# A moving operand's high and low parts laid side by side: one run of 512 values where there were two of 256

## The reference

```python
def first_block(...):
    h = concatenate([m, x], axis=1)
    h = h + hybrid_mixer(rmsnorm(h, norm_mix), w_in, ..., w_out)
    h = h + swiglu(rmsnorm(h, norm_ffn), w_gate, w_up, w_down)
    return rmsnorm(h, final_norm)[:, N_META:]

def second_block(...):
    h = x @ w_in                    # q, k, v, u and two gates
    ...
    merged = sigmoid(gate_attn) * y_attn + sigmoid(gate_pool) * y_pool
    x = layer_norm(ALPHA * x + merged @ w_out)
    return layer_norm(ALPHA * x + square(relu(x @ w_ff1)) @ w_ff2)
```

## Time and profile before

| | |
|---|---|
| median of 3 runs | 2449.61 us (2449.36 to 2449.77) |
| the profiled execution: time, span | 2449.89 us, 2447.8 us |
| TensorE matmuls, busy | 2433.8 us, 99%, 14762 matmuls |
| VectorE, busy | 1614.5 us, 66% |
| ScalarE, busy | 1202.2 us, 49% |
| GpSimd, busy | 173.9 us, 7% |
| share of the SP queue's transfers | 58.8% of 16 DMA engines |
| read from HBM | 445.12 MB |

### The profile page before, as it was taken

How to read it: one execution, slowest core, us unless ns; L and a number is a source line. 1 busy time by engine, 2 the same in 40 slices (tenths; PEclk the granted TensorE clock), 3 DMA queues, 4 the chain that set the end, 5 groups by cost and what they waited for, 6 DMA issues and landing times.

```text
span 2447.8 us, 36417 instructions
## 1 busy us (share of the span) xinstructions
PE 2433.8 (99%) x14762; PEld 2173.7 (89%) x14762; DVE 1614.5 (66%) x2518; ACT 1202.2 (49%) x1728; POOL 173.9 (7%) x195
## 2 busy tenths in 40 slices
PE   8999999999999999999999999999999999999999
PEld 8999998888888888888888888888998888888887
DVE  5646676676666666667677756678885665565667
ACT  6545545544544543455555654544554443443544
POOL 0001111000000000002211102031110000000010
PEclk9999999999999999999999999999999999999999
DMA  7554456666566666665655455565566666656663
GB/s 250 180 161 139 141 165 189 200 184 194 182 198 190 189 190 189 192 190 185 197 188 167 166 185 190 184 193 186 162 196 193 189 189 189 194 190 189 183 193 117
DMA packets 125751, 449.59 MB, mean 184 GB/s; under 512 B 13840, under 2 KB 16400, under 8 KB 125584
## 3 DMA queue, kind: packets, MB, share of 16 engines
q1 hardware_dynamic: 125296, 446.91, 58.8%
q10 hardware_dynamic: 288, 0.36, 0.0%
HBM read 445.12 MB, written 2.10 MB: 183 GB/s over the span
## 4 chain that ended last, share of the span: by engine, by line
PE 96%; DVE 2%; ACT 1%; issue 0%; DMA 0%; ACTq 0%
PE out_bank L614 28%; PE out_bank L618 27%; PE out_bank L615 14%; PE out_bank L617 14%; PE out_bank L622 3%; PE out_bank L621 3%; PE out_bank L623 3%; DVE w_lo L1307 1%; ACT w_hi L895 0%; PE side_bank L734 0%; PE side_bank L694 0%; PE side_bank L749 0%; PE side_bank L725 0%; DVE h L1824 0%; DMA h<-in_tokens 0%
## 5 line engine op out<-in xcount | busy, mean ns | idle before, releaser
L1307 DVE TENSOR_TENSOR w_lo<-raw,w_hi 128x1024 fp32r<-128x1024 f32 x839 | 1037.4, 1240 | 601.0 <-ACT w_hi L895 596.9
L895 ACT CAST w_hi<-raw 128x1024 fp32r<-128x1024 f32 x840 | 878.1, 1049 | 953.6 <-PE out_bank L618 874.8
L614 PE MATMUL out_bank<-a_op,w_hi 128*128 128x512 f32 x1984 | 784.2, 395 | 0.5 <-DVE h L1334 0.3
L618 PE MATMUL out_bank<-a_op,w_hi 128*128 128x512 f32 x1984 | 776.7, 391 | 0.0
L615 PE MATMUL out_bank<-a_op,w_lo 128*128 128x256 f32 x1984 | 558.8, 282 | 0.0
L617 PE MATMUL out_bank<-a_op,w_lo 128*128 128x256 f32 x1984 | 552.0, 278 | 0.0
L617 PEld LDWEIGHTS out_bank<-a_op,w_lo 128*128 128x128 f32 x1984 | 380.1, 192 | 84.3
L615 PEld LDWEIGHTS out_bank<-a_op,w_lo 128*128 128x128 f32 x1984 | 372.9, 188 | 77.0
L614 PE MATMUL out_bank<-b_op,w_hi 128*128 128x512 f32 x992 | 389.7, 393 | 0.0
L618 PE MATMUL out_bank<-b_op,w_hi 128*128 128x512 f32 x992 | 388.0, 391 | 0.0
L614 PEld LDWEIGHTS out_bank<-a_op,w_hi 128*128 128x128 f32 x1984 | 373.1, 188 | 2.0 <-DVE w_lo L1307 0.7
(11 more groups left out here) (302 smaller groups left out, 1974.6 us busy)
## 6 DMA issues: line engine op xcount, KB each, us to landing
raw<-in_w_ff SPq DMA_DIRECT2D x256, 512.0 KB, 4.2
raw<-in_w_in SPq DMA_DIRECT2D x223, 512.0 KB, 3.7
raw<-in_w_gu SPq DMA_DIRECT2D x176, 512.0 KB, 4.2
raw<-in_w_down SPq DMA_DIRECT2D x88, 512.0 KB, 4.3
raw<-in_w_out SPq DMA_DIRECT2D x64, 512.0 KB, 4.3
raw<-in_w_ba SPq DMA_DIRECT2D x16, 512.0 KB, 3.9
raw<-in_w_bp SPq DMA_DIRECT2D x16, 512.0 KB, 3.8
out<-h SPq DMA_DIRECT2D x8, 256.0 KB, 2.3
```

Of the source, the lines that this page charges most:

```text
L614: t_.e.matmul(bank[:, :], wh, a_both, start=start, stop=False, skip_group_check=True)
L618: mm = t_.e.matmul(bank[:, :], wh, a_both, start=False, stop=stop, skip_group_check=True)
L895: a.e.copy(w_hi[:, m % SPLIT, :], raw[:, u % RAW, :]).then_inc(hi_split)
L1307: v_.e.tensor_tensor(w_lo[:, m % SPLIT, :], raw[:, u % RAW, :], w_hi[:, m % SPLIT, :].bitcast(F32), ALU.subtract).then_inc(lo_split)
```

## The change

In `a_late` the low part's 256 columns now lie directly behind the high part's. The high rows of both K tiles of a slot begin where they began (values 48 and 564 of the slot); the low rows begin at values 304 and 820 instead of 306 and 822. The 512-column in-products of the late stages read one run of 512 values; those of 256 columns read the high row as before. `b_op`, the early stages, the count and the order of all instructions and all waits are the same.

```diff
+        def side_by_side(kt, i):
+
+            at = PLACE + ROW * 2 * (kt % 2) + SEQ * i
+            return a_late[:, kt // 2, at:at + SEQ * (2 - i)]
+
             def moving(blk, cols, kt):
 
                 if blk.operand == "a" and blk.stage not in ("k", "f", "q", "v", "conv"):
-                    return part(a_late, kt, 0), part(a_late, kt, 1), parts(a_late, kt)
+                    return side_by_side(kt, 0)[:, 0:SEQ], side_by_side(kt, 1), side_by_side(kt, 0)
...
-                            v_.e.scalar_tensor_tensor(part(a_late, j, 1), h[:, j, REAL], p_col(gain, j),
+                            v_.e.scalar_tensor_tensor(side_by_side(j, 1), h[:, j, REAL], p_col(gain, j),
                                                       part(a_late, j, 0).bitcast(F32), ALU.mult,
                                                       ALU.subtract).then_inc(norm_split)
...
-                v_.e.tensor_tensor(part(a_late, j, 1), src, part(a_late, j, 0).bitcast(F32),
+                v_.e.tensor_tensor(side_by_side(j, 1), src, part(a_late, j, 0).bitcast(F32),
                                    ALU.subtract).then_inc(merged_split)
...
-                    v_.e.tensor_tensor(part(a_late, slot, 1), work[slot % 4][:, 0:SEQ],
+                    v_.e.tensor_tensor(side_by_side(slot, 1), work[slot % 4][:, 0:SEQ],
                                        part(a_late, slot, 0).bitcast(F32), ALU.subtract).then_inc(ff_split)
```

## The result

The changed kernel takes **2472.69 us** (2472.51 to 2472.86, 3 runs) against 2449.61 us: 23.1 us slower, a ratio of 1.0094 with a 95% interval of 1.0071 to 1.0117. The forecast was no change, and the time lies 15.7 us above the range.

The account below looks back on a forecast made before the run. The prediction took TensorE's own pace to bound the kernel, 1856 cycles of 693.3 ns being 53% of the span. Its terms summed 0 + 0 + 0, so it forecast no change, 2449.6 us, with a range of 2438 to 2457 us.

Parts of the forecast that it names:

- What bounds the kernel, and the pace of a cycle: TensorE, busy 2433.8 of 2447.8 us, sets the time; 1856 affected cycles of four in-products take 693.3 ns each.
- something other than the layout: Suspected if the second operand's stages or `q`, which the change leaves alone, did not keep 693 ns a cycle.
- Point 1: TensorE's 512-column reads become one run: a jump costs at most 2.4 ns, saving up to 8.8 us; taken as 0.
- The bound from the one-run reads of `k`: Stage `k`'s 272-column one-run matmuls have 12.1 ns excess each, leaving at most 4.7 ns a cycle for two jumps.
- Point 2: Low rows of the late operand begin 8 bytes earlier: a start's place was said not to matter; taken as 0.
- Point 3: VectorE writes the low rows 8 bytes earlier: at worst 5.6 us if slower and uncovered; taken as 0.
- point 4: What would bind next: were TensorE 1% faster, no other bound, such as the making of weights, would be met.
- Rival B: TensorE's moving-operand and weight reads fall on each other otherwise: 7 ns a cycle slower, 2462.6 us; chance 0.15.
- the sign that only the gaps of 512 columns would carry the loss: In TensorE's starts, a gain or loss should show in each 512-column gap and not in the 256-column ones.
- Rival A: Each jump in TensorE's long reads costs 2.4 ns: 2440.8 us, chance 0.17; far more, under 2438, chance 0.07.
- Rival C: TensorE joins or splits runs itself, so 8 bytes are nothing to it: forecast time; chance 0.61 together with the forecast.
- The lines of 16 bytes: SBUF said to be read in 16-byte lines; one line fewer per low row would save 6.6 us; not adopted.

Follow-up runs that it names:

- e1: The changed kernel with only the even K tiles' low rows directly behind the high ones, the odd ones keeping their 8-byte jump: 2473.02 us.
- e2: The changed kernel with only the odd K tiles' low rows directly behind the high ones, the even ones keeping their 8-byte jump: 2473.11 us.
- e3: The changed kernel with all low rows 16 bytes behind the end of the high ones, so two runs per long read: 2463.06 us.
- e10: The changed kernel with the odd K tile's rows 16 bytes earlier (2240, 3264), all long reads still in one run: 2449.2 us.
- e7: The changed kernel with 64 bytes of padding ahead of the weight buffers: 2479.56 us.
- e8: The kernel before the change with 64 bytes of padding ahead of the weight buffers: 2496.54 us.
- e13: The changed kernel with 128 bytes of padding ahead of the weight buffers, the column of `minus` placed in the padding: 2439.29 us.
- s2_scan: The changed kernel with seven late-operand layouts, one for each time it is written; 693.3 ns a cycle in `gu`, 686.7 in steady `out2`; no total given.
- e12: The changed kernel with every row of the late operand 128 bytes earlier (starts 64 and 2128): 2438.67 us.

## Why the prediction was wrong

- *What bounds the kernel, and the pace of a cycle*: right. TensorE's own pace was the whole matter, 1856 cycles carried it, and the other operand kept its pace. `q` kept its time, but not its pace at every moment (700.0 ns where 693.2 had been read), which the prediction had named as a sign of something other than the layout.
- *Point 1, the jump costs between 0 and 2.4 ns*: wrong in kind. The jump has no price of its own. It moves the low row, and that made -6.7 or +3.3 ns a jump at the two places tried. The bound from the one-run reads of `k` compared two widths at two places as if they were two forms of reading, and so was no bound.
- **Point 2 is the step that failed**: "Three layouts, two kinds of alignment, two lengths of jump, one pace: I take 0 here too." The term was put at 0 and measured 13.3 ns a cycle over 1856 cycles. Of the three layouts, two are the same (late layout and `b_op`), and `q` was read on 19 cycles that end where its pace goes to 700. Moved by 64 bytes against the weights, the kernel before goes at 710.0. A place that two stages share is one sample, not two. Behind it stood a tacit assumption, that only alignment within the row could matter; nothing asked where the weights lie.
- *Point 3 and point 4*: right; no wait on the low parts' writes appeared, and at 686.8 ns nothing else came to bind.
- *Rival B* had the mechanism, reads of the moving operand and of the weights that fall on each other otherwise, and the warning sign, single gaps that differ between `gu` and `q`. Its price, 7 ns a cycle (up to 10), was half of the 13.3 measured; it had been given a chance of 0.15. The reason against it, that the low half lies behind the weight load, fell with e1 and e2: 8 bytes in one low row move the gaps of all kinds of in-product, those of 256 columns too (115.0 to 123.3 ns in e2). So did the sign that only the gaps of 512 columns would carry the loss: in the changed kernel 4.5 of the 13.3 ns are in the others.
- *Rival A* as a fixed price is refuted by e3 and e10. *Rival C* is refuted by the result.
- One rule that bears on rival B was not weighed. By the Trainium skill (TensorE: Matmul & The Clock Gate, Part 2, step 1), moving operand and weight load have read ports of their own, and loading the next tile's weights takes no read bandwidth from the running matmul. By that rule no padding ahead of the weights should change a pace, yet the pace of `gu` went from 706.6 to 700.1 ns (e7), from 693.3 to 710.0 (e8) and from 706.6 to 686.8 (e13). The measurement decides: the two reads are not independent here.
- The lines of 16 bytes that the prediction took from the Trainium skill (Advanced Engine Details and Errata, Memory Cachelines) don't tell fast from slow: e3 has all starts on line boundaries and is slower than before.

**What stays open.** Shown is that the pace depends on the place of the moving rows against the weight buffers, that a move of one or of the other is the same, and that the writing of the weights has no part in it. The dependence seems to repeat: slots are 4352 bytes apart (17 x 256) and weight tiles 512, and in the kernel before neither changes the pace, so the period seems to divide 256 bytes, while 64, 16 and 8 bytes matter. How TensorE's two reads hinder each other is open, and so is what picks one of two paces at the same place (`q`, s2_scan, e12, e13). No rule was found that gives the pace of an untried place, and it wasn't searched whether one under 686.7 exists. `b_op` was left at its place, so what it could gain was not tried.

## What to carry to other kernels

Where TensorE is the bound and its start-to-start times lie above columns over clock (here 693 ns for 640), try the addresses: shift the moving operand or the weight buffers by 16, 64 and 128 bytes, and read the pace in one profiled run, over long stretches of several stages: within a steady stretch it repeats to the nanosecond, but a place can have two paces. Judge an edit of layout only after re-tuning its place: the change here is worth +23 us or -11 us with the same reads. And a stage that agrees with another is evidence only if it differs in what could matter; several layouts can be tried in one kernel, one to each stage.

## What was not expected of the hardware

- 64 bytes of padding ahead of two buffers, with no instruction changed, cost 46 us of 2450 (e8_w64_before): 2496.54 against 2450.28 us.
- Over all places tried, a cycle of 1536 columns with four weight loads took 686.7 to 713.3 ns, against 640 ns at 2.4 GHz. Most steady means lie on steps: 686.7, 690.0, 693.3, 696.7, 700.0, 706.7, 710.0, 713.3, all multiples of 3.33 ns. One doesn't: 697.8 in s2_scan (0/2272), with a beat over three cycles.
- Slow places often have a beat over two output tiles (697 and 716 ns in the changed kernel), though both tiles read the same rows. In e1_even the beat is over three cycles (696, 702 and 722 ns), which no address of the four weight tiles follows, and in e2_odd, as slow, there is none.
- With one and the same layout the pace can be 693.3 or 706.7 ns for over 80 cycles in a row (s2_scan).
